# Recurrence layers: cross products and block attention interleaved, square roots as exp(-ln/2), row sums of block 1 at other places

## What is computed

```
for l in range(2):
    x = x + 0.5 * swiglu_ffn(rms_norm(x), ...)
    proj = rms_norm(x) @ w_mix_in[l]
    y_rwkv = rwkv7_time_mix(proj[..., :RWKV_PROJ], ...)     # 8 heads of 64
    y_moba = moba_attention(q_m, k_m, v_m, rel_bias)        # 8 heads of 64
    x = x + concat([y_rwkv, y_moba]) @ w_mix_out[l]
    x = x + memory_cross_attention(rms_norm(x), rms_norm(mem), ...)
    x = x + 0.5 * swiglu_ffn(rms_norm(x), ...)

rwkv7_time_mix:
    kk = kk / max(sqrt(sum(kk * kk)), 1e-12);  b = kk * a
    per step: state = state * w + (state @ -kk) b^T + v k^T;  y = state @ r
    y = (y - mean) * rsqrt(var + LNX_EPS) * ln_g + ln_b
    y = (y + sum(r * k * r_k) * v) * g
```

## Time and profile before

| | |
|---|---|
| median of 3 runs | 2569.61 us (2569.6 to 2573.0) |
| the profiled execution, its time | 2570.07 us |
| its span in the trace | 2567.9 us |
| TensorE matmul busy | 2424.4 us (94%) |
| VectorE busy | 617.1 us (24%) |
| ScalarE busy | 349.7 us (14%) |
| mean granted clock of TensorE | 0.974 of full speed |

### The profile page before, as it was taken

One profiled execution on the slowest core, in us unless ns is written; L12 is line 12 of the kernel. 1 busy time (PEld: TensorE's weight loads), 2 busy tenths in 40 slices (PEclk: granted clock), 3 DMA queues, 4 the chain that ended last, 5 costly groups with the idle time before them and its releaser, 6 DMA issues. The chain is left out here.

```text
span 2567.9 us, 29161 instructions
## 1 busy us (share of the span) xinstructions
PE 2424.4 (94%) x12476; PEld 1663.2 (65%) x12476; DVE 617.1 (24%) x1212; ACT 349.7 (14%) x658; POOL 43.9 (2%) x74
## 2 busy tenths in 40 slices
PE   7899979999999899998989999999999898999998
PEld 5678744444444677787575677777777766567775
DVE  2788221111111200033362110010003146311001
ACT  1123221111111100012212110000001221221000
POOL 1000000000000000000000000000000000000000
PEclk9899979999999899999989999999999998999999
DMA  9556649999999544453312144444444422124442
GB/s 388 204 210 249 251 102 383 422 422 422 422 422 422 181 147 147 147 180 131 111 56 99 50 140 152 160 159 144 159 159 169 143 82 84 66 66 156 147 147 82
DMA packets 176134, 499.46 MB, mean 194 GB/s; under 512 B 7192, under 2 KB 99624, under 8 KB 146096
## 3 DMA queue, kind: packets, MB, share of 16 engines
q1 hardware_dynamic: 172224, 481.23, 49.9%
q0 software_dynamic: 3680, 16.43, 2.2%
q10 hardware_dynamic: 144, 0.52, 0.1%
HBM read 491.34 MB, written 6.82 MB: 194 GB/s over the span
## 5 line engine op out<-in xcount | busy, mean ns | idle before, releaser
L1957 PE MATMUL bank<-xT,ring 128*128 128x256 f32 x2816 | 617.0, 380 | 0.0
L1957 PEld LDWEIGHTS bank<-xT,ring 128*128 128x128 f32 x2816 | 535.9, 191 | 88.3 <-issue 17.2
L1971 PE MATMUL bank<-ring,fh 128*128 128x512 f32 x704 | 308.6, 592 | 0.0
L1971 PEld LDWEIGHTS bank<-ring,fh 128*128 128x128 f32 x704 | 133.8, 190 | 151.3 <-issue 149.2
L2570 DVE TENSOR_TENSOR fs<-bank,R 128x512 f32<-128x512 f32 x44 | 30.4, 691 | 772.2 <-PE bank L1957 772.2
L2006 PE MATMUL bank<-xT,ring 128*128 128x256 f32 x704 | 152.6, 379 | 0.0
L834 PE MATMUL bank<-xT,ring 128*128 128x256 f32 x640 | 147.4, 391 | 2.8 <-ACT xT L278 2.8
L2006 PEld LDWEIGHTS bank<-xT,ring 128*128 128x128 f32 x704 | 133.4, 190 | 18.0
L834 PEld LDWEIGHTS bank<-xT,ring 128*128 128x128 f32 x640 | 125.6, 197 | 23.5 <-ACT xT L278 2.9
L2382 ACT ACTIVATE fs<-fs 128x512 f32<-128x512 f32 x44 | 27.7, 629 | 801.0 <-DVE fs L2570 801.0
L1369 PE MATMUL bank<-ring,xg 128*64 128x512 f32 x512 | 114.6, 594 | 8.1 <-DMA ring<-in_w 8.1
(11 more groups left out here) (432 smaller groups left out, 2242.1 us busy)
## 6 DMA issues: line engine op xcount, KB each, us to landing
ring<-in_w SPq DMA_DIRECT2D x128, 1024.0 KB, 19.0
ring<-in_ffn_w_in SPq DMA_DIRECT2D x88, 1024.0 KB, 7.7
ring<-in_first_pieces SPq DMA_DIRECT2D x33, 2048.0 KB, 12.2
more<-in_w SPq DMA_DIRECT2D x64, 1024.0 KB, 19.5
ring<-in_ffn_w_out SPq DMA_DIRECT2D x44, 1024.0 KB, 5.0
ring<-in_w_mix_in SPq DMA_DIRECT2D x12, 2048.0 KB, 8.8
ring<-in_xattn_w_kv SPq DMA_DIRECT2D x8, 2048.0 KB, 11.2
ring<-in_w_mix_out SPq DMA_DIRECT2D x4, 2048.0 KB, 9.8
```

Source lines behind the costliest of these rows:

```text
L1957: last = nc.tensor.matmul(bank[2 * par + u][:, c * SEQ:(c + 1) * SEQ], w[:, k, m:m + P], xT[:, k, :], start=(k == 0), stop=(k == KD - 1))
L1971: last = nc.tensor.matmul(bank[4 + 2 * half + t][:, :], fh[:, par, c * SEQ + t * P:c * SEQ + (t + 1) * P], w[:, c, half * 512:(half + 1) * ...
```

## The change

It has three parts. In the mixer of both layers, cross products 0 and 2, both with their two halves, are made ahead of the first head of the block attention, with the bonus row sums before them; cross products 1 and 3 are made a half at a time behind heads 0 to 3, in one bank; and VectorE takes them out between its logits and probabilities, with the beginning of the inverse (`inverse_start`). `cross_kv` groups 0, 1, 2 and 3 are spread around these, and groups 5 to 7 are cut in halves over heads 1 to 6. The wait for the stores `k_stored` and `v_stored` moves from TensorE ahead of cross product 0 to ScalarE ahead of its copy of cross product 4. The row sums for the norm of `kk` move into the projection (after group 11), and banks change to suit.

Roots are exp(-ln/2) on ScalarE, with no reciprocal on VectorE, for the norm of `kk` and for the group norm; the group norm's last product is done in two halves.

In the first block three `ada_mm` stand behind later projection groups, and `ada_take` behind other work of VectorE. GpSimd has one more memset at the start, for the constant `lnx_eps`.

The diff, cut to its core:

```diff
             after = {g: [] for g in range(G_N)}
-            for i, g in enumerate((1, 3, 5, 7, 10)):
+            for i, g in enumerate((1, 5, 6, 8, 10)):
...
                                         cz[:, 2 * p:2 * p + 2, :], ALU.mult).then_inc(proj_dve, 1)
-                ada_take(4 + p)
 
             dve.wait_ge(proj_dve, 2)
             convolve(8)
+            ada_take(4)
             ada_sum(7)
+            ada_take(5)
             for p in range(2):
                 if p:
                     convolve(4)
                 dve.wait_ge(proj_full, G_K + p + 1)
                 nc.vector.tensor_copy(flat(kT[:, 2 * p:2 * p + 2, :]), bank[(G_K + p) % NB][:, :]).then_inc(proj_dve, 1)
-                ada_take(6 + p)
+            ada_take(6)
             ada_sum(8)
             for p in range(2):
...
             dve.wait_ge(proj_dve, 6)
+            ada_take(7)
+            convolve(3)
             ada_take(8)
...
-        MAT_BANK = [0, 4, 2, 6] + [4, 6] * 5
+
+        MAT_BANK = [2, 3, 6, 3] + [4, 6] * 5
+        MAT_POS = [0, 2, 1, 3] + list(range(4, 14))
         N_MAT, N_MDVE, N_MACT, N_INV, N_U = 28, 20, 8, 10, 8
 
         def mats_by_dve(idx):
 
-            return 2 * idx + 2 if idx < 4 else 2 * (idx - 4) + 2
+            return 2 * MAT_POS[idx] + 2 if idx < 4 else 2 * (idx - 4) + 2
+
+        def mat_bank(idx, e):
+            return bank[MAT_BANK[idx] + (0 if idx in (1, 3) else e)]
+
+        def mat_done(l, idx, e):
+            return l * N_MAT + 2 * MAT_POS[idx] + e + 1
...
+                if m == 11:
+                    pe.wait_ge(kk_sq, l + 1)
+                    pe.wait_ge(proj_dve, l * MP_DVE + (len(BY_DVE) + 8))
+                    for n in range(2):
+                        nc.tensor.matmul(bank[6 + n][:, :], K[:, HEADS, :], flat(cw[:, 2 * n:2 * n + 2, :]),
...
+                    if g in (3, 4):
+                        pe.wait_ge(proj_act, l * MP_ACT + (len(BY_ACT) + g - 2))
...
-                pe.wait_ge(kk_sq, l + 1)
-                for n in range(2):
-                    nc.tensor.matmul(bank[6 + n][:, :], K[:, HEADS, :], flat(cw[:, 2 * n:2 * n + 2, :]),
-                                     start=True, stop=True).then_inc(heads_psum, 1)
-
-                pe.wait_ge(lora_act, l * N_LORA + 6)
+                pe.wait_ge(kk_ss, (l + 1) * 2)
                 for t in range(NT):
                     for m in range(4):
-                        last = nc.tensor.transpose(bank[2 + t][:, m * P:(m + 1) * P],
+                        last = nc.tensor.transpose(bank[6 + t][:, m * P:(m + 1) * P],
...
+            def cross_kv(l, g, parts=(0, 1)):
+
+                if 0 in parts:
+                    if g < 2:
+                        pe.wait_ge(lora_act, l * N_LORA + (g + 1))
+                    else:
+                        pe.wait_ge(kv_act, l * 8 + (g - 1))
...
+                    for part in parts:
+                        for k in range(4 * part, 4 * part + 4):
+                            last = nc.tensor.matmul(bank[g % 2][:, :], gm[:, k, t * P:(t + 1) * P], w[:, k, :],
+                                                    start=(k == 0), stop=(k == KD - 1))
...
-                pe.wait_ge(kv_act, (l + 1) * 8)
                 pe.wait_ge(rk_ready, l + 1)
                 for n in range(2):
-                    nc.tensor.matmul(bank[n][:, :], K[:, HEADS, :], flat(cw[:, 2 * n:2 * n + 2, :]),
+                    nc.tensor.matmul(bank[6 + n][:, :], K[:, HEADS, :], flat(cw[:, 2 * n:2 * n + 2, :]),
                                      start=True, stop=True).then_inc(heads_psum, 1)
...
+            def mats(l, idx, es=(0, 1)):
...
+                if idx == 2:
+                    pe.wait_ge(bonus_ready, l + 1)
+                elif idx in (6, 7, 8, 9):
+                    pe.wait_ge(mat_act, l * N_MACT + mats_by_act(idx - 2))
+                elif idx >= 10:
+                    pe.wait_ge(mat_dve, l * N_MDVE + mats_by_dve(idx - 2))
+                lhs, lc_, rhs, rc_ = MATS[idx]
+                if idx in (1, 3):
+                    pe.wait_ge(mat_dve, l * N_MDVE + (idx + 3 + es[0]))
+                    for e in es:
+                        rows_ = slice(e * HD, (e + 1) * HD)
+                        for m in range(4):
+                            last = nc.tensor.matmul(mat_bank(idx, e)[:, m * P:(m + 1) * P],
+                                                    f(lhs, m, (c0, c1)[lc_], rows_), f(rhs, m, (c0, c1)[rc_], rows_),
+                                                    start=True, stop=True)
+                        last.then_inc(mat_full, 1)
+                    return
...
-                pe.wait_ge(kk_ss, (l + 1) * 2)
                 pe.wait_ge(lora_act, (l + 1) * N_LORA)
                 scores(0)
                 scores(1)
-                pe.wait_ge(gm_ready, l + 1)
-                for g in range(4):
-                    cross_kv(l, g)
+                cross_kv(l, 1)
+                bonus(l)
+                cross_kv(l, 2)
+                pe.wait_ge(fac_ready, l + 1)
+                mats(l, 0)
+                mats(l, 2)
+                cross_kv(l, 3)
+                fill = {0: [(4, 0), (4, 1)], 1: [(5, 0)], 2: [(5, 1)], 3: [(6, 0)], 4: [(6, 1)], 5: [(7, 0)], 6: [(7, 1)]}
                 for h in range(NH):
+                    if h == 0:
+                        pe.wait_ge(mat_dve, l * N_MDVE + 4)
                     turned(h)
                     if h + 2 < NH:
                         scores(h + 2)
+                    if h == 4:
+                        pe.wait_ge(mat_dve, l * N_MDVE + 8)
                     values(h)
+                    for g, part in fill.get(h, ()):
+                        cross_kv(l, g, (part,))
                     if h < 4:
-                        cross_kv(l, 4 + h)
+                        mats(l, 1 + 2 * (h // 2), (h % 2,))
...
-                pe.wait_ge(fac_ready, l + 1)
-                pe.wait_ge(k_stored, (l + 1) * 16)
-                pe.wait_ge(v_stored, (l + 1) * 16)
...
+                for idx in range(4, 8):
+                    mats(l, idx)
                 pe.wait_ge(mb_oc, (l + 1) * 2)
-                pe.wait_ge(bonus_ready, l + 1)
...
+                pe.wait_ge(gm_ready, l + 1)
+                cross_kv(l, 0)
                 moba_attention(l)
-                bonus(l)
...
-                for n in range(2):
-                    act.wait_ge(kk_ss, l * 2 + (n + 1))
-                    t = flat(bon[:, 2 * n:2 * n + 2, :])
-                    nc.scalar.activation(t, t, ACT.Sqrt).then_inc(kk_rs, 1)
+                    if m == 12:
+                        continue
+
+                    for n in range(2):
+                        act.wait_ge(kk_ss, l * 2 + (n + 1))
+                        t = flat(bon[:, 2 * n:2 * n + 2, :])
+                        st(nc.scalar.activation(t, t, ACT.Ln))
+                    st.sync()
+                    for n in range(2):
+                        t = flat(bon[:, 2 * n:2 * n + 2, :])
+                        nc.scalar.activation(t, t, ACT.Exp, scale=-0.5).then_inc(kk_rs, 1)
...
-                    if 1 <= h <= 4:
-                        take_kv(3 + h)
+                    if h % 2:
+                        take_kv(4 + h // 2)
...
+                act.wait_ge(k_stored, (l + 1) * 16)
+                act.wait_ge(v_stored, (l + 1) * 16)
...
-                    act.wait_ge(gn_var, l * 2 + (n + 1))
+                    act.wait_ge(heads_psum, l * N_HEADS + (n + 7))
+                    st(nc.scalar.activation(xs[:, 1, n * 512:(n + 1) * 512], bank[2 + n][:, :], ACT.Ln,
+                                            scale=1.0 / HD, bias=lnx_eps[:, 0:1]))
+                st.sync()
+                for n in range(2):
                     t = xs[:, 1, n * 512:(n + 1) * 512]
-                    nc.scalar.activation(t, t, ACT.Sqrt).then_inc(gn_rs, 1)
+                    nc.scalar.activation(t, t, ACT.Exp, scale=-0.5).then_inc(gn_rs, 1)
                 for k in range(4):
...
-                st(nc.vector.reciprocal(flat(bon[:, :, :]), flat(bon[:, :, :])))
-                st.sync()
...
+                def inverse_start(ch):
+                    dve.wait_ge(mat_dve, l * N_MDVE + 2 * ch + 6)
...
+                dve.wait_ge(bias_loaded, 16)
+                dve.wait_ge(mem_loaded, 64)
+                logits(0)
+                for h in range(NH):
+                    if 1 <= h <= 4:
+                        ch, e = (h - 1) // 2, (h - 1) % 2
+                        diagonal(2 * ch + 1, e, X, C_LEV)
+                        if e == 1:
+                            inverse_start(ch)
+                    if h + 1 < NH:
+                        if h >= 1:
+                            dve.wait_ge(at_t, l * N_AT + h)
+                        logits(h + 1)
+                    probs(h)
+                    if h == 0:
+                        for n in range(2):
+                            dve.wait_ge(heads_psum, l * N_HEADS + (n + 3))
```

(31 more changed lines are left out.)

98 lines of the change are left out of this document (33 added, 65 removed).

## The result

The changed kernel takes 2591.66 us (median of 4, 2589.99 to 2596.51) against 2569.61: ratio 1.0086, interval 1.0069 to 1.0104. It is slower by 22 us (18 to 27); forecast were 11, in a range from 2561 to 2593. The profiled execution took 2590.27 us, 20.2 more than the profiled one of before.

A forecast was written before the change was run, and what follows sets the result against it. TensorE, busy 94%, was taken as the bound, so only waits and clock count. Per layer 14.4 - 6.4 - 1.3 = 6.7 worse, 13.4 for two, less 2 in block 1: 11.4 on 2570.07, 2581 us; range 2561 to 2593.

The forecast's parts named there:

- mechanism of the heads: Heads 1 to 4: TensorE waits for probabilities behind the half cross product, 2.95 twice and 4.97 twice, 15.9 us per layer.
- the forecast's own 2575 to 2587: Whole kernel: range of the case "forecast as worked out", 2581 us, chance 0.45.
- Clock in the heads: Heads 1 to 4: clock falls behind each of four waits, 2.7 us each, 10.8 per layer.
- Clock behind the bonus: Behind cross product 2's wait for the bonus products: clock loss of 0.8 us per layer.
- Cross products in halves: Cross products 1 and 3, a half at a time: no term in the sum; only waits and clock were to count.
- The store: Values' store ahead of cross products 4 and 6: landing takes 9.6 us, TensorE idles 9.25 per layer.
- The stretch as a whole: Mixer, projection's end to the inverse's first round: 44.0 us of new losses against 29.6, 14.4 worse per layer.
- Group norm and cross attention: Group norm: shorter TensorE wait and kept clock, 6.4 us better; cross attention: no table load, 1.3 better, per layer.
- Block 1: First block: the group at 76.73 can start 2.5 us earlier, some comes back; taken as -2 (-3 to 0).
- The root of kk: Factors ahead of cross product 0: the 6.54 us reciprocal goes from their chain; cost 0 to 0.6, taken as 0.

The follow-up runs named there:

- the halves ahead of the fill: Changed kernel with the half cross products of heads 0 to 3 moved ahead of the filling cross_kv products: 2542.03 us, ratio 0.9902.
- the split store: Changed kernel with the store of the values in two halves of 512 KB, the first issued earlier: 2587.97 us, ratio 1.0079.
- Noff last: Changed kernel with Noff made last of ScalarE's four copied products and the wait for the values' store moved ahead of that copy: 2577.64 us, ratio 1.0030.
- the experiment with the loads held: Changed kernel with the two xattn_w_q weight loads started only after the store of the values has landed: 2588.44 us, ratio 1.0076.
- the final order: Changed kernel with Noff last, head 0's exponential ahead of group 2's copy, cross products 1 and 3 whole ahead of head 0: 2504.63 us, ratio 0.9754.

## Why the prediction was right, and where its sum was off

It was right in direction, and in place and size of nearly every wait: 2.91 and 4.96 against 2.95 and 4.97, 8.6 against 9.25, 2.4 against 3.0, 1.9 against 1.9, `xT` at 0.49. The mechanism of the heads is shown by moving two lines. The measured time lies 10.7 us above the forecast, 1.3 under the range's upper end and outside the forecast's own 2575 to 2587, so it is the wide range that holds it; the terms missed or too small nearly all pulled the same way. The sum 2 x 2.95 + 2 x 4.97 is 15.84, not 15.9, which changes nothing. By steps:

**Clock in the heads**, taken at 2.7 per wait: 3.1 (12.4 a layer against 10.8). The waits of 2.9 had a fall behind them in both layers, though 2.75 in the earlier trace rows had none.

**Clock behind the bonus**, taken at 0.8: 1.7 (a spell of 3.4 us at 0.50), though that wait is shorter than the one of 2.75. It isn't a fixed price. Cross product 2 and the filling group behind it in layer 1, first in the changed kernel, then with the halves ahead of the fill, where this part of the layer is the same:

```profile
2077.70 1.16 PE L2128 MATMUL bank<-aT,kk 64*128 64x128 f32 x16 [2.45 <-DVE bon L2821]
2078.79 8.86 PE L2082 MATMUL bank<-gm,ring 128*128 128x256 f32 x32
```

```profile
2054.24 1.16 PE L2128 MATMUL bank<-aT,kk 64*128 64x128 f32 x16 [2.45 <-DVE bon L2821]
2055.33 7.17 PE L2082 MATMUL bank<-gm,ring 128*128 128x256 f32 x32
```

The same wait of 2.45 us had a fall behind it in the first and none in the second. It had none either in layer 1 of the runs with the split store and with Noff last.

**Cross products in halves**: not in the sum. The prediction took a half at half of a whole; it takes the same 1.16 us. 2.2 a layer.

**The store**: 8.6 and 10.0 where 9.25 were taken. That it is late because of its company is shown by the experiment with the loads held.

**The stretch as a whole**: predicted 14.4 a layer worse. It grew by 16.45 and 18.25, and the row sums of 1.75 have left it, so 18.2 and 20.0. The terms above explain 28.7 + 12.4 + 1.7 + 2.3 + 2.2 - 29.6 = 17.7 of the 18.2, and 1.4 of layer 1's further 1.8 is its longer wait for the store.

**Group norm and cross attention**, taken at 6.4 and 1.3: 6.2 and 6.1 by the stages, and 1.0. The first of the two table loads (before the logarithm) is hidden in an idle time of ScalarE, the second is the 1.28 us shown above, as the prediction took it. The Trainium skill ("ScalarE: Activation LUTs", section "Table sets: the hidden batching unit") gives about 2.7 us for a load and one load for ln and then exp; by its section "What ACT_TABLE_LOAD costs", 1.283 of the 2.7 is the load and the rest a drain. The trace agrees with the 1.283. It shows no drain: the load starts 0.02 behind the second logarithm and the exponential 0.01 behind the load. And two loads ran, not one. That a load left the cross attention gave 1.0 of its 1.28, since TensorE's wait there is 1.71 where it was 2.75.

**Block 1**, taken at -2: 0, or 0.4 at most. Its price was read from one place, where a later wait gave it back.

**The root of kk**, taken at 0: in the final order it is worth 5.9 a layer by the medians. By itself in the changed kernel it wasn't tried.

The sum by these is 38.2 - 12.3 - 2.0 = 23.9, and the two profiled spans differ by 20.6. Of this, -3.9 arose ahead of the mixer stretch of layer 0, which begins at 1188.93 against 1191.10, though 1.75 of row sums now stand before it. Of these, 1.5 is the first group's start; the rest isn't assigned. It is within the spread: in the traces of the versions, with the same code up to there, this point lies anywhere from 1188.2 to 1194.4.

## What to carry to other kernels

A product whose result an engine must take out before its next urgent work belongs ahead of the filling work, not behind it: 50 us lay in the order of two lines. When work is spread over slots, ask of each slot which queue its extraction stands in, and who waits for the instruction behind it. A change of several parts should be timed by part: here +37 hid -15. A difference of 2 us between absolute times of one pair of traces isn't an effect: count from an event that both share.

## What the runs showed of the hardware

Two 64-row halves of a product that are issued in turn into two banks take 1.16 us together; one half alone takes 1.16 as well. From start to the start of what follows, it is 0.99 (1309.38 to 1310.37) for the pair in the changed kernel, and 1.08 to 1.09 for the half with the halves ahead of the fill.

A wait of 2.45 us was followed by a fall of the granted clock to 0.50 in both layers of the changed kernel and by none in layer 1 of three of its versions; one of 2.75 was not the earlier trace rows. The length of a single wait didn't decide, nor did the products around it, which were the same.

A store of 1 MB landed in 5.4 us alone and 9.2 beside 4 MB of loads; half of it took 2.9 alone and, beside the same loads, still 8.1 to 8.8. By the Trainium skill ("DMA: Bandwidth & Descriptors", section "Anatomy of one DMA — SWDGE (gpsimd) path"), which has about 2.0 us plus the bytes over 436 GB/s, 1 MB is an estimated 4.4 us; this case's 5.4 is a little above.

TensorE, otherwise without waits, had gaps by "issue" of up to 2.3 us with Noff last while loads filled the queues or just after. Why isn't shown.
